# The sample rows of a body's two head pairs as one unit, and outputs dealt to three visits in the last bodies

## What is computed

```
xp = xp + 0.5 * swiglu_ffn(xp, *ffn1)
xs = xs + 0.5 * swiglu_ffn(xs, *ffn1)
op, sp = mixer_prompt(rmsnorm(xp, norm_gains[l, 1]), *lw)
os_, ss = mixer_sample(rmsnorm(xs, norm_gains[l, 1]), cache_a_k[l], ..., *lw)
xp = xp + op
xs = xs + os_
...
def attend(q, k, v, bias, mask, sinks):
    s = jnp.einsum('btkgd,blkd->bkgtl', qg, k).astype(jnp.float32) * ATTN_SCALE
    s = s + bias ...
    p = softmax(s)            # group B: a learned sink in the sum too
    o = jnp.einsum('bkgtl,blkd->btkgd', p.astype(v.dtype), v)
```

## Time and profile before

| | us |
|---|---|
| median of 3 runs | 1931.11 (1930.79 to 1931.24) |
| the profiled execution, its own time | 1930.58 |
| its span in the trace | 1929.0 |
| PE busy in the span | 1919.9 |
| DVE, ACT, POOL busy | 1169.8, 847.5, 88.4 |
| waits of PE that the trace names | 6.4 in 11 waits |

### The profile page before, as it was taken

The page is one execution under the profiler, slowest core; times in us unless marked ns, Lnnn a source line. Parts: engine busy times, 40 slices in busy tenths (PEclk is TensorE's granted clock), DMA queues, the critical chain, the costliest instruction groups (busy, mean ns, idle before and its releaser), DMA issues.

```text
span 1929.0 us, 41891 instructions
## 1 busy us (share of the span) xinstructions
PE 1919.9 (100%) x15805; PEld 1899.6 (98%) x15805; DVE 1169.8 (61%) x1790; ACT 847.5 (44%) x1290; POOL 88.4 (5%) x140
## 2 busy tenths in 40 slices
PE   9999999999999999999999999999999999999999
PEld 8999999999999999999998999999999999999999
DVE  7555445555455566599889766555445555455554
ACT  7433334333343345345668644444334333343332
POOL 0000000000000000023432000000000000000000
PEclk9999999999999999999999999999999999999999
DMA  7555555555555555554553455555555555555564
GB/s 270 181 174 171 184 184 179 174 171 185 188 174 174 176 170 187 183 165 150 162 163 116 141 178 184 180 174 171 183 186 178 174 171 184 188 174 175 175 195 157
DMA packets 101275, 339.98 MB, mean 176 GB/s; under 512 B 12149, under 2 KB 16293, under 8 KB 101200
## 3 DMA queue, kind: packets, MB, share of 16 engines
q1 hardware_dynamic: 95856, 329.41, 52.2%
q0 software_dynamic: 2960, 7.45, 1.4%
q10 hardware_dynamic: 2400, 2.33, 0.4%
HBM read 334.45 MB, written 5.28 MB: 176 GB/s over the span
## 4 chain that ended last, share of the span: by engine, by line
PE 94%; DVE 4%; ACT 1%; issue 1%; DMA 0%; SPq 0%; DVEq 0%; ACTq 0%
PE bank L607 31%; PE bank L608 30%; PE bank L609 30%; DVE w_lo L1378 1%; PE bank L696 1%; PE bank L729 1%; PE bank L711 0%; PE bank L673 0%; DMA raw<-in_w_ffn_gate 0%; DVE s_buf L1459 0%; DVE s_buf L1495 0%; DVE p_t L1607 0%; DVE top L1605 0%; ACT s_buf L1122 0%; PE bank L911 0%
## 5 line engine op out<-in xcount | busy, mean ns | idle before, releaser
L607 PE MATMUL bank<-h_hi_and_lo,w_hi 128*128 128x288 f32 x3344 | 962.1, 288 | 1.6 <-DVE w_lo L1635 1.1
L608 PE MATMUL bank<-h_hi_and_lo,w_hi 128*128 128x288 f32 x3344 | 957.2, 286 | 0.0
L609 PE MATMUL bank<-h_hi_and_lo,w_lo 128*128 128x288 f32 x3344 | 957.1, 286 | 0.0
L1378 DVE TENSOR_TENSOR w_lo<-raw,w_hi 128x1024 fp32r<-128x1024 f32 x634 | 729.6, 1191 | 203.0 <-ACT w_hi L1065 202.6
L1065 ACT ACTIVATE w_hi<-raw 128x1024 fp32r<-128x1024 f32 x634 | 616.4, 1019 | 289.9 <-PE bank L609 282.9
L607 PEld LDWEIGHTS bank<-h_hi_and_lo,w_hi 128*128 128x128 f32 x3344 | 632.6, 189 | 6.7 <-DVE w_lo L1635 2.8
L608 PEld LDWEIGHTS bank<-h_hi_and_lo,w_hi 128*128 128x128 f32 x3344 | 632.8, 189 | 0.2
L609 PEld LDWEIGHTS bank<-h_hi_and_lo,w_lo 128*128 128x128 f32 x3344 | 632.7, 189 | 0.0
L609 PE MATMUL bank<-gu_hi_and_lo,w_lo 128*128 128x288 f32 x1376 | 393.5, 286 | 0.0
L608 PE MATMUL bank<-gu_hi_and_lo,w_hi 128*128 128x288 f32 x1376 | 393.5, 286 | 0.0
L607 PE MATMUL bank<-gu_hi_and_lo,w_hi 128*128 128x288 f32 x1376 | 393.5, 286 | 0.0
(11 more groups left out here) (205 smaller groups left out, 985.4 us busy)
## 6 DMA issues: line engine op xcount, KB each, us to landing
raw<-in_w_ffn_gate SPq DMA_DIRECT2D x168, 512.0 KB, 4.5
raw<-in_w_ffn_up SPq DMA_DIRECT2D x168, 512.0 KB, 4.6
raw<-in_w_ffn_down SPq DMA_DIRECT2D x96, 512.0 KB, 3.7
raw<-in_w_in SPq DMA_DIRECT2D x74, 512.0 KB, 4.7
raw<-in_w_ffn_down SPq DMA_DIRECT2D x64, 384.0 KB, 4.2
raw<-in_w_out SPq DMA_DIRECT2D x32, 512.0 KB, 4.5
raw<-in_w_ffn_down SPq DMA_DIRECT2D x32, 448.0 KB, 4.3
bias_rev<-bias_vectors POOLq DMA_DIRECT2D x11, 256.0 KB, 4.8
```

The source lines that it names most:

```text
L607: pe.matmul(out, w_hi[b][:, k, :], hi, start=(k == first_k), stop=False)
L608: pe.matmul(out, w_hi[b][:, k, :], lo, start=False, stop=False)
L609: mm = pe.matmul(out, w_lo[b][:, k, :], hi, start=False, stop=(k == last_k))
L1378: dve.tensor_tensor(w_lo[b][:, k, :], raw_tile(ph, j, s)[:, k, :], w_hi[b][:, k, :].bitcast(F32), ALU.subtract)\
```

## The change

The two pairs' sample rows become one unit. The queries of four heads stand in one tile, 32 columns for each head, with zeros elsewhere (`sample_place`), so that two matmuls on 128 partitions, the second adding to the first in one bank, give the scores of all four heads in 128 rows by 160 keys. A body has five units: 0 and 1 of pair 0, 2 and 3 of pair 1, and 4 the samples. Scale, bias, maximum, exponential, division, transposition and copy are one instruction (or two) for all four. The values stay eight small matmuls. The sums of squares of the samples are one pair of matmuls into one column (`mean_any`) in place of two with two columns. POOL now squares and places the samples' queries in pieces of 64 partitions by 32 columns, each behind a wait for the one before, and loads a bias of their own (`bias_s`) with four DMAs a body. The bias of pair 1 moves behind both placements, and the cached keys behind the bias. Outputs are read after units 0 and 1 (256 columns), and after unit 4 the rest.

```diff
+        UNITS = 5
+        PAIR_OF, ROWS_OF = (0, 0, 1, 1, None), (0, 1, 0, 1, 2)
+        S_COL = 8
+        S_OUT = [slice(NT, NT + T_S), slice(T_P, NT)]
+        def sample_place(p, c):
+            return slice(c * HD, (c + 1) * HD), slice(T_P + T_S * (2 * p + c), T_P + T_S * (2 * p + c + 1))
...
-            return (2 * v, 2 * v + 1) if 0 <= v < 12 else ()
+            return [v // 3 * UNITS + u for u in ((0, 1), (2, 3), (4,))[v % 3]] if 0 <= v < 12 else []
...
-            return [group * 6 + u for u in ((0, 1), (2,), (3, 4, 5))[part]] if v >= 2 else []
+            return [group * UNITS + u for u in ((0, 1), (2, 3), (4,))[part]] if v >= 2 else []
...
+            def scores(U, u, q, kt):
+                b, r = u % 2, ROWS_OF[u]
+                if b == 0 and not (isinstance(U, int) and U + u < 1):
+                    pe.wait_ge(s_add, U + u)
                 if r == 2:
-                    settled()
...
+                    for p in range(2):
+                        mm = pe.matmul(bank_s[0][:, 0:NKEY[r]], q[p][:, FULL[r]], kt[p][:, KEY0[r]:KEY0[r] + NKEY[r]],
+                                       start=(p == 0), stop=(p == 1))
...
                 if r == 2:
-                    settled()
...
+                    pe.transpose(bank_t[b][:, 0:P], s_buf[slot][:, 0, 0:P], ident[:, :])
+                    mm = pe.transpose(bank_t[b][0:T_S, P:2 * P], s_buf[slot][:, 0, P:P + T_S], ident[:, :])
...
+                    for p in range(2):
+                        for kc in range(2):
+                            for c in range(2):
+                                at = T_S * (2 * p + c)
+                                mm = pe.matmul(bank_o[c * HD:(c + 1) * HD, S_OUT[p]], v[p][:, 2 + kc, cols[c]],
+                                               p_t[2][:, kc, at:at + T_S], start=(kc == 0), stop=(kc == 1))
...
                 tp(0)
                 tp(1)
                 piece(2)
+                sc(4)
+                tp(2)
                 tp(3)
-                sc(4)
-                sc(5)
-                tp(2)
-                for u in range(3):
-                    pv(u)
+                pv(0)
+                pv(1)
                 piece(3)
                 tp(4)
                 set_sums(*sums)
-                tp(5)
-                for u in range(3, 6):
+                for u in range(2, 5):
                     pv(u)
...
+                for p in range(2):
+                    for c in range(2):
+                        first = T_S * (2 * p + c)
+                        pool.dma_start(bias_s[first:first + T_S, :], win_s[kinds[p]][c][at]).then_inc(bias_s_ld, 16)
...
+            def place_sample_q(b, gains):
+                if not (isinstance(b, int) and b == 0):
+                    pool.wait_ge(qk_done, b * UNITS)
+                    settled()
+                for p in range(2):
+                    for c in range(2):
+                        rows, cols = sample_place(p, c)
+                        ins = pool.tensor_scalar(q_wide[p][rows, cols], z_q[p][rows, T_P:NT], qk_cols[rows, gains[p]:gains[p] + 1], ATTN_SCALE,
+                                                 ALU.mult, ALU.mult)
+                        if c == 0:
+                            ins.then_inc(q_step, 1)
+                            pool.wait_ge(q_step, b * 6 + (5 + p))
+                            settled()
+                    ins.then_inc(qs_rdy, 1)
...
-                pool.tensor_tensor(sq_set[which], z[:, :], z[:, :], ALU.mult).then_inc(set_sq, 1)
+                pool.tensor_tensor(sq_wide[1 + p][:, 0:T_P], z[:, 0:T_P], z[:, 0:T_P], ALU.mult).then_inc(q_step, 1)
+                for c in range(2):
+                    pool.wait_ge(q_step, b * 6 + (2 * p + 1 + c))
+                    settled()
+                    rows, cols = sample_place(p, c)
+                    ins = pool.tensor_tensor(sq_wide[1 + p][rows, cols], z[rows, T_P:NT], z[rows, T_P:NT], ALU.mult)
...
+                if project == "a":
+                    place_q(b, 1, b * 2 + (a_ph.n0 - 10 + 2), a_squares(b, 1), 0)
+                place_sample_q(b, (4, 2) if project == "cb" else (0, 0))
+                if nxt:
+                    load_bias(nxt[1], at, 1, b)
+                    load_sample_bias(nxt, at, b)
                 if nxt and nxt[0] == "c":
-                    pool.wait_ge(pv_done, U + 3)
+                    pool.wait_ge(pv_done, U + UNITS)
                     settled()
                     place_c_cache(at)
```

More of the change, by code:

```diff
@@ L670, in set_sums @@
                 for p in pairs:
-                    for r in range(3):
+                    for r in range(2):
                         c = NT + scale_col(p, r)
                         mm = pe.matmul(misc_bank(m)[:, c:c + 2], sq_wide[1 + p][:, FULL[r]], mean_hd2[:, :], start=True, stop=True)
+                if pairs[-1] == 1:
+                    for p in range(2):
+                        c = NT + S_COL
+                        mm = pe.matmul(misc_bank(m)[:, c:c + 2], sq_wide[1 + p][:, FULL[2]], mean_any[:, :], start=(p == 0), stop=(p == 1))
                 mm.then_inc(m_done, 1)
@@ L681, in turn_rows @@
                 pe.transpose(misc_bank(m)[0:width, 2 * P:3 * P], tile[:, T_P:T_P + width], ident[:, :]).then_inc(m_done, 1)
-            def settled():
-                pe.sem_inc(pe_passed, 1)
-            def scores(U, r, b, q, kt, paired):
-                if not (paired and b == 1) and not (isinstance(U, int) and U < 1):
-                    pe.wait_ge(s_add, U)
-                if r == 2:
-                    settled()
-                for c in range(2):
-                    half = slice(c * HD, (c + 1) * HD)
-                    mm = pe.matmul(bank_s[c][:, b * T_P:b * T_P + NKEY[r]], q[half, FULL[r]],
-                                   kt[half, KEY0[r]:KEY0[r] + NKEY[r]], start=True, stop=True)
-                mm.then_inc(qk_done, 1)
@@ L1480, in smax @@
                     dve.wait_ge(mx_raw, c0 + 2)
-                    dve.tensor_tensor(snk[b][0:m, :], nmax[b][0:m, :], ns, ALU.subtract).then_inc(mx_rdy, 1)
+                    dve.tensor_tensor(snk[b][rows, heads], nmax[b][rows, heads], ns, ALU.subtract).then_inc(mx_rdy, 1)
             def inverse(kind, body, u):
-                b, r, p = u % 2, u % 3, u // 3
-                slot = s_slot(body * 6, u)
-                m = ROWS[r]
-                dve.wait_ge(e_rdy, body * 6 + (u + 1))
-                if kind == "cb" and p == 1:
-                    dve.tensor_tensor(esum[b][0:m, :], esum[b][0:m, :], esnk[b][0:m, :], ALU.add).then_inc(sum_sunk, 1)
+                b, r, p = u % 2, ROWS_OF[u], PAIR_OF[u]
@@ L1490, in inverse @@
+                slot = s_slot(body * UNITS, u)
+                heads = slice(0, 1 if r == 2 else 2)
+                dve.wait_ge(e_rdy, body * UNITS + (u + 1))
+                if kind == "cb" and p != 0:
+                    rows = slice(HD, P) if r == 2 else slice(0, P)
+                    dve.tensor_tensor(esum[b][rows, heads], esum[b][rows, heads], esnk[b][rows, heads], ALU.add).then_inc(sum_sunk, 1)
                     dve.wait_ge(sum_sunk, body * 3 + (r + 1))
-                dve.reciprocal(einv[b][0:m, :], esum[b][0:m, :]).then_inc(r_rdy, 1)
@@ L1492, in inverse @@
[L1492 removed]
+                dve.reciprocal(einv[b][:, heads], esum[b][:, heads]).then_inc(r_rdy, 1)
+                dve.wait_ge(r_rdy, body * UNITS + (u + 1))
                 n = NKEY[r]
[L1494 to L1495 removed]
+                for c in range(1 if r == 2 else 2):
+                    ins = dve.tensor_scalar(s_buf[slot][:, c, 0:n], s_buf[slot][:, c, 0:n], einv[b][:, c:c + 1], None, ALU.mult)
@@ L1514, in attention_pairs @@
+                    for u in units:
+                        smax("cb", body, u)
+                    reads[j]()
+                    for u in units:
+                        inverse("cb", body, u)
+                    if j == 2:
+                        out_lo(body, 0, tiles)
+                    if j == 3:
                         set_inverses(*sums)
@@ L1539, in last_bodies @@
                     j, k = divmod(v, 3)
-                    g0, g1 = run_scored(v)
+                    units = [unit(g) for g in run_scored(v)]
                     if k == 0 and j:
                         scales(MISC_A0 + 2 * j - 1, 0, j + 4)
-                    smax(*unit(g0))
                     if k == 1 and j:
                         scales(MISC_A0 + 2 * j, 1, j + 4)
-                    smax(*unit(g1))
-                    if k < 2 and j:
-                        out_lo(j + 3, k, run_tile(j + 3, k))
+                    for at in units:
+                        smax(*at)
+                    if k == 2:
+                        out_lo(j + 4, 0, [run_tile(j + 4, p) for p in range(2)])
+                    elif k == 1 and j:
+                        out_lo(j + 3, 1, [run_tile(j + 3, p) for p in range(2)])
                     if k == 2 and 0 < j < 3:
```

343 lines of the change are left out of this document (195 added, 148 removed).

## The result

The changed kernel takes 1934.21 us (median), the kernel before 1931.2: a ratio of 1.0016, 95% interval 1.0009 to 1.0022. So it is slower by 3 us, within 0.2% of no change. The forecast was 1925.4 with a range from 1921.8 to 1930.0.

A forecast was written before the change was run, and what follows sets the result against it. TensorE, busy 1919.9 of 1929.0 us, was taken as the bound. Work −4.9, waits −1.3 and POOL +0.5 gave −5.7: 1924.9 from the profiled 1930.58, 1925.4 with 0.5 for the median; range 1921.8 to 1930.0.

The forecast's parts named there:

- rival 3: Bodies 5 to 7: pair 1's bias, loaded behind both placements, up to 1.2 us late; +2.4 at most, 1927.8; chance 0.10.
- rival 4: Body 4: with less work on DVE the granted clock's fall goes too, −1.7 us, 1923.7; chance 0.10.
- The cushion: Bodies 6 and 7: TensorE's transposes follow 6 us after DVE needs the bias, and DVE had 0.39 idle there.
- The price of a small piece: POOL's 64 by 32 pieces: 0.15 us each plus 0.17 for the wait before, taken from a 64 by 128 fill.
- rival 1: POOL late in every loop body, 1.0 to 1.5 us at the sums; +3 to +4.5, 1928 to 1929.5; chance 0.14.
- TensorE's work: Samples' scores, transposes and values save 0.54 us a body, 4.3 for eight; taken as 4.9, bounds 3.2 and 6.5.
- TensorE's waits: Body 0's wait goes, −0.6; body 7's goes, −1.0, with +0.3 for the last output reads; body 4 unchanged; sum −1.3.
- DVE is ready no earlier: Body 4's third visit: the transposes' 0.69 us wait for DVE and the clock's fall stay, charged 0, −1.7 as a bound.
- GpSimd in the loop bodies: POOL adds 4.8 us a body against 4.9 of room; sums of bodies 1 to 3 charged +0.5, bounds 0 and 4.5.
- Rival 2: Bodies 0 to 3: waits at the sums, each followed by a clock fall; +6.2, 1937; chance 0.05, shared with others above 1935.
- the chances: Stated odds for the whole kernel: faster (below 1927.2) 0.70, same (1927.2 to 1935) 0.23, slower 0.07.

The follow-up runs named there:

- the kernel with the early load: Changed kernel with pair 1's bias load in bodies 4 to 7 issued before the squares of pair 1: 1923.13 us, 0.9958 to the kernel before.
- the repaired kernels: Changed kernel with pair 1's bias load in bodies 4 to 7 moved before pair 1's squares (1923.13 us) or between its queries and the placements (1922.3 us).
- the kernels with the load early or between: Changed kernel, pair 1's bias load in bodies 4 to 7 before pair 1's squares (1923.13 us), or between its queries and the four placements (1922.3 us).
- the late order there: Kernel before, with pair 1's bias load in bodies 4 to 7 issued behind the queries of pair 1: 1931.9 us, 1.0001.
- the best kernel: Changed kernel with pair 1's bias early in bodies 4 to 7 and, in bodies 0 to 3, GpSimd's own work done while biases land: 1921.7 us, 0.995.
- the two experiments on the kernel before: Kernel before with pair 1's bias load behind its queries in bodies 4 to 7: 1931.9 us; the same plus six small GpSimd steps ahead: 1932.16 us.
- the wait put back: Changed kernel with pair 1's bias early, plus four unread VectorE copies ahead of the divisions in body 4's second visit: 1923.26 us, 0.996.
- the latest load: Changed kernel with pair 1's bias load in bodies 4 to 7 issued behind the four DMAs of the samples' bias too: 1942.12 us, 1.0056.

## Why the prediction was wrong

**The size of rival 3.** This is the step that failed. The sum charged nothing for the bias of pair 1, and rival 3, which named it, priced it at +2.4 at most and gave it 0.10. It put four terms on one line, and for body 6 they measured:
- From the read of `z_q` to the issue: 4.0 to 5.4 predicted, 6.6 measured. The squares of a pair took 2.29 with their steps (0.69, 0.18, 1.00, 0.18, 0.24), where 1.24 stood; the placements 2.14, where 1.1 stood; the step to the DMA 0.86, where 0.3 stood.
- The landing: 4.8 predicted, the median of eleven; 5.6 measured, and 5.8 to VectorE's first use.
- The need: 9.0 to 9.5 predicted, about 8.9 measured.
- Late by up to 1.2, predicted; 5.8 + 6.6 − 8.9 = 3.5 measured, and in the same way 2.9 in body 5, which the prediction held to be free of it, and 4.3 in body 7, where VectorE itself was free only at 1072.65.

Body 5 has a reason of its own. In the kernel before its bias was needed 10.5 us after the read of `z_q` (1021.65 to 1032.14), because the strip between body 4's third group and the next ran in part at the lower clock: it took 5.68 us there and 4.00 in the changed kernel. With the fall of rival 4 gone, the need came 8.7 us after the read.

Everything came through: the groups lost 2.6, 3.3 and 5.0 us against the kernel with the early load, 10.9 with some 1.2 of the clock's fall in it, and 0.5 more in the strip behind, 11.4 where +2.4 was the most that was priced. (The two spans are 12.2 apart; the kernel's start differs by 1.5, the fourth groups by −1.0.) The cushion that the prediction named, that the transposes follow 6 us later, was no help, because TensorE does not wait at the transposes first: the samples' scores of the next piece wait for the bank that VectorE reads with the bias, and the outputs, the divisions and `w_lo` are queued behind that read.

**The price of a small piece.** It is the error inside the first of those terms, and it was taken from a fill. GpSimd's groups in the changed kernel, with count, total us and mean ns:

```profile
L2007 POOL TENSOR_TENSOR z_prep<-z_q 64x32 f32<-64x32 f32 x32 | 15.9, 497 | 5.7 <-POOL z_prep L2002 2.9 <-POOL z_prep L2007 2.9
L1974 POOL TENSOR_SCALAR q_n<-z_q,qk_cols 64x32 f32<-64x32 f32 x32 | 12.4, 386 | 7.1 <-POOL q_n L1974 4.8 <-POOL q_n L1962 2.3
```

Undisturbed such a piece takes 0.23 to 0.29, not 0.15, and the means are 0.50 and 0.39. Of the 64 pieces eleven took 1.00 to 2.22, and every one of these ran beside a `w_lo`; another ten, beside VectorE's scaling, masks or divisions, took 0.33 to 0.48. The piece at 1042.91 that took 1.00 ran beside VectorE's `w_lo` (1042.18, 1.64 us long). The prediction had the rows for that, the cached keys' copy, and used them against rival 1 alone; the sum of rival 3 had no blocked step in it but one of the queries. By the Trainium skill's page "GPSIMD Engine Reference" (Specifications), which the prediction cited, pieces that meet an instruction with two SBUF inputs contend with it; the trace agrees (1.00 beside `w_lo`, 0.24 for the same piece behind it), and the rule belonged in this sum too.

**TensorE's work** was right. A loop body's four groups were 1.28 + 1.63 + 2.53 + 3.12 = 8.56 and are 1.28 + 1.58 + 2.10 + 3.05 = 8.01 where no wait disturbs them, so 0.55 a body against 0.54 predicted. By parts: scores 0.55 (0.63 predicted), transposes 0.14 (0.2), values 0.54 (0.48).

**TensorE's waits.** Body 0's and body 7's old ones went, as predicted. Body 4's went too, against the prediction's words that "DVE is ready no earlier". VectorE was ready 0.9 us earlier, counted from the last strip product ahead of the group (1017.30 − 1014.24 = 3.06 before, 1015.71 − 1013.51 = 2.20 now). It began the divisions 0.6 sooner, and the second one is shorter: before, the samples' stood first and took 0.91 as two, the 256-key unit's 0.81 behind it; now the 256-key unit stands first (0.91) and the 128-key unit behind it takes 0.48. The third group of body 4 went from 4.08 to 2.78, and the clock stayed up: −1.3 and −1.7, of which 0 and 0 were taken. That is rival 4, given 0.10. It, the wait and the work explain why the repaired kernels are at 1922 to 1923 and not at the forecast's 1925.4.

**GpSimd in the loop bodies.** Its idle time before the keys' squares fell from 4.67 to 0.5 and 0, below 1 as predicted, and the sums of bodies 1 to 3 waited 0.27, 0.14 and 0.25, in all 0.7 where +0.5 was charged. One more wait of this kind was not in the sum: in body 7 the sums (L692) waited 0.61 for GpSimd's small squares, and 0.38 in the kernels with the load early or between. Rival 1's 1.0 to 1.5 a body did not come; the most seen in any run was 0.96, once. Rival 2's falls of the clock in bodies 0 to 3 did not come. In the kernel before they can: in the trace of the late order there, a wait of 0.84 for the outputs in body 0 was followed by 3.4 us at 0.50 (from 901.25), where the 0.58 of the kernel before left the clock up.

Together, on the spans: −9.2 for the best kernel (1929.0 to 1919.8). Its groups give −2.8 in bodies 0 to 3, −1.4 in body 4, −3.6 in bodies 5 to 7, and the clock −1.7: −9.5; the stretches before and behind the bodies took 0.3 more. The changed kernel had nearly all of this gain and gave it back, and 3 us more, at one DMA.

One slip is in the chances: by their own parts they add up to 0.69 faster, 0.26 the same and 0.05 slower, not 0.70, 0.23 and 0.07. Nothing hangs on it.

## What to carry to other kernels

When a change puts steps ahead of a load on a queue, write the load's whole line (steps, issue, landing, need) with every step at its dearest seen value, and check it for each consumer that the change also moves earlier; two small shifts that are each harmless can meet. A bias load has no reason to stand behind arithmetic that it does not depend on: start it as soon as its buffer is free, and do the arithmetic while it lands. And if a changed kernel comes out level, look for a gain and a loss, not for nothing.

## What the runs showed of the hardware

- GpSimd's operation on 64x32 elements costs 0.23 to 0.29 us undisturbed and 1.0 to 1.4 beside a split of VectorE (once in each trace of the new order 2.22), with 0.18 to 0.36 from one step to the next, and 0.72 to 0.92 to a DMA behind it.
- The same load of 256 KB lands 3.5 to 6.6 us after its issue, once 8.8 (110 loads in ten traces), and 3.5 to 3.8 where the strips' queue moves next to nothing. The four small DMAs behind it have no part in that; that the strips' transfers cause it is likely, not shown.
- The granted clock is not told by one wait. In the three profiles with the old order it fell between 1010 and 1030 us (0.96 and 0.87; in the two experiments on the kernel before 1.00 and 0.83), with TensorE busy 9.0 of the first 10. With the new order it stayed at 1.00 at 9.03 of 10 and the wait put back. The changed kernel was even busy only 8.06 between 1030 and 1040 and 7.91 between 1050 and 1060 with the clock at 1.00; the latest load brought 7.05 and 0.74. Where the clock falls it stands at 0.50 for 3.4 us in most cases, 1.7 us lost, and for 10.2 and 6.8 with the latest load. What distinguishes the first case stays open.
